# Dealing an expert's rows over all 128 partitions, and moving the small blocks as half rows

## The reference

```
top_val, top_idx = lax.top_k(logits, TOP_K)          # 4 of 32 experts for each of 512 tokens
top_w = jax.nn.softmax(top_val, axis=-1)
...
xb = h_pad[tok]                                      # rows of one expert
gu = xb @ w1[e] + b1[e]                              # 1024 -> 2048
gate = jnp.minimum(gate, SWIGLU_LIMIT)
up = jnp.clip(up, -SWIGLU_LIMIT, SWIGLU_LIMIT)
act = (up + 1.0) * (gate * jax.nn.sigmoid(SWIGLU_ALPHA * gate))
yb = act @ w2[e] + b2[e]                             # 1024 -> 1024
out = out.at[buf_tok].add(yb * wts)                  # back to the tokens
```

## Time and profile before

| | |
|---|---|
| median of 3 runs | 1963.04 us (1961.03 to 1964.29) |
| the profiled execution | 1963.06 us, span 1960.8 us, granted clock 0.99 |
| PE busy | 1857.0 us, 95% of the span |
| DVE, ACT, POOL busy | 1102.3, 942.7, 417.1 us |
| moved by DMA | 511.61 MB, mean 261 GB/s |

### The profile page before, as it was taken

The page is one execution under the profiler, slowest core; times in us unless marked ns, Lnnn a source line. Parts: engine busy times, 40 slices in busy tenths (PEclk is TensorE's granted clock), DMA queues, the critical chain, the costliest instruction groups (busy, mean ns, idle before and its releaser), DMA issues. The chain is left out here.

```text
span 1960.8 us, 27519 instructions
## 1 busy us (share of the span) xinstructions
PE 1857.0 (95%) x8716; PEld 1308.4 (67%) x8716; DVE 1102.3 (56%) x1354; ACT 942.7 (48%) x1342; POOL 417.1 (21%) x423
## 2 busy tenths in 40 slices
PE   7999999999999999997999999999999999999997
PEld 5887887887887888786655665556545655565553
DVE  6657657757757333456753564355445554564456
ACT  5666666666666222325443544344434443444341
POOL 0412421321320000012021233123322232223110
PEclk9999999999999999997999999999999999999998
DMA  5122122122131222366999999999999999999997
GB/s 182 65 89 87 65 88 99 54 88 99 64 108 57 97 97 96 131 238 230 369 403 415 414 403 402 409 409 405 402 411 405 405 404 406 407 402 404 406 397 325
DMA packets 88062, 511.61 MB, mean 261 GB/s; under 512 B 12882, under 2 KB 15994, under 8 KB 37720
## 3 DMA queue, kind: packets, MB, share of 16 engines
q1 hardware_dynamic: 80728, 492.70, 64.0%
q0 software_dynamic: 6720, 16.35, 2.4%
q10 hardware_dynamic: 576, 2.10, 0.3%
HBM read 502.08 MB, written 24.46 MB: 269 GB/s over the span
## 5 line engine op out<-in xcount | busy, mean ns | idle before, releaser
L2295 DVE TENSOR_TENSOR w_lo<-big,w_hi 128x2048 fp32r<-128x2048 f32 x141 | 322.1, 2292 | 354.3 <-ACT w_hi L2009 354.2
L2009 ACT ACTIVATE w_hi<-big 128x2048 fp32r<-128x2048 f32 x141 | 268.8, 1916 | 384.5 <-DMA big<-in_w 357.3
L1776 PE MATMUL bank<-big,keep 128*64 128x512 f32 x896 | 204.1, 600 | 0.0
L1197 PE MATMUL bank<-h_hi,wm_hi 128*128 128x512 f32 x416 | 171.1, 411 | 3.9 <-DVE big L918 2.4
L1197 PE MATMUL bank<-h_hi,wm_lo 128*128 128x512 f32 x416 | 163.0, 392 | 0.0
L1197 PE MATMUL bank<-h_lo,wm_hi 128*128 128x512 f32 x416 | 162.2, 390 | 0.0
L2295 DVE TENSOR_TENSOR w_lo<-keep,w_hi 128x2048 fp32r<-128x2048 f32 x48 | 110.0, 2294 | 71.4 <-ACT w_hi L2009 69.9
L1756 PE MATMUL bank<-w_hi,x_hi 128*128 128x512 f32 x512 | 144.0, 403 | 3.8 <-DVE w_lo L2295 3.2
L1776 PEld LDWEIGHTS bank<-big,keep 128*64 128x64 f32 x896 | 60.2, 137 | 118.8 <-issue 118.8
L1756 PE MATMUL bank<-w_lo,x_hi 128*128 128x512 f32 x512 | 137.6, 390 | 0.0
L1756 PE MATMUL bank<-w_hi,x_lo 128*128 128x512 f32 x512 | 137.1, 389 | 0.0
(11 more groups left out here) (352 smaller groups left out, 3711.1 us busy)
## 6 DMA issues: line engine op xcount, KB each, us to landing
big<-in_w SPq DMA_DIRECT2D x289, 1024.0 KB, 15.4
keep<-in_w SPq DMA_DIRECT2D x95, 1024.0 KB, 14.2
big<-in_w_mix SPq DMA_DIRECT2D x72, 512.0 KB, 3.3
keep<-in_w_tail SPq DMA_DIRECT2D x44, 512.0 KB, 3.2
big<-y_tok SPq DMA_DIRECT2D x5, 1024.0 KB, 11.7
keep<-in_x SPq DMA_DIRECT2D x8, 512.0 KB, 6.6
keep<-y_tok SPq DMA_DIRECT2D x3, 1024.0 KB, 10.5
big<-in_w_tail SPq DMA_DIRECT2D x4, 512.0 KB, 3.7
```

The costliest lines, as they stand in the source:

```text
L1197: ins = pe.matmul(to[:], w[:, k], h[:, k], start=(k == 0 and w is hi and h is h_hi), stop=(k == KT - 1 and w is lo))
L1776: ins = pe.matmul(bank[2 * (c // 2)][r, :], x_s[:, n], raw[s][:, c * 512:(c + 1) * 512], start=False, stop=n == KT - 1)
L2009: act.activation(w_hi[:, s], raw[r], ACT.Copy).then_inc(hi_ready, 1)
L2295: dve.tensor_tensor(w_lo[:, s], raw[r], w_hi[:, s].bitcast(F32), ALU.subtract).then_inc(lo_ready, 1)
```

## The change

`CAP` becomes 128, so a big block has a slot in each partition. The number of a slot no longer is its partition's: `slot_no` is filled by an iota of four dimensions, which deals the rows out. Partition 64a + 32b + 4c + d (a, b in 0 and 1; c in 0 to 7; d in 0 to 3) gets slot number 1 + 8a + 64b + c + 16d. So rows 1 to 8 go to partitions 0, 4, ..., 28, rows 9 to 16 to 64, 68, ..., 92, rows 17 to 24 to 1, 5, ..., 29, and so on; rows 1 to 64 fill partitions 0 to 31 and 64 to 95, and rows from 65 on the other half.

A small block is gathered as 128 half rows of 2 KB: left halves to partitions 0 to 63, right halves to 64 to 127, each dealt in the same manner. Its eight transposes become four. Its results go out in one DMA of 128 half rows. Three small tables (`row_half`, `y_half_row`, `small_row`) hold the numbers for this; DVE fills them. The memsets of the edge from slot 112 to 128 go away, and the small DMA that doubled `cols` at the end, too. With blocks of 128 the overflow has 16 blocks at most, not 20.

```diff
-CAP, CS = 112, 64
+CAP, CS = 128, 64
-NOV = 20
+NOV = 16
+SMALL_ROWS = [(slice(32 * n, 32 * n + 32), slice(64 * (n % 2), 64 * (n % 2) + 32)) for n in range(4)]
...
+        h2_half = h2_rows.rearrange("r (h n) -> (r h) n", h=2)
...
                 def turn_x_s(b):

-                    for k in range(KT):
-                        ins = pe.transpose(bank[6][:, k * CS:(k + 1) * CS], xg_s[:, k * P:(k + 1) * P],
-                                           ident[0:CS, 0:CS])
+                    for k in range(4):
+                        ins = pe.transpose(bank[6][:, k * P:(k + 1) * P], xg_s[:, k * P:(k + 1) * P], ident)
...
+                for n, (to, of) in enumerate(SMALL_ROWS):
+                    ins = dve.tensor_scalar(row_half[to], rows[of, 0:E], 2.0, float(n // 2), ALU.mult, ALU.add)
+                ins.then_inc(halves_ready, 1)
...
-                    dve.tensor_scalar(halves[:, 0], slots[0:CS, 0:E], 2.0, None, ALU.mult)
-                    dve.tensor_scalar(halves[:, 1], slots[0:CS, 0:E], 2.0, 1.0, ALU.mult, ALU.add).then_inc(halves_ready, 1)
+                    for n, (to, of) in enumerate(SMALL_ROWS):
+                        dve.tensor_copy(small_row[to], rows[of, 0:E])
+                        ins = dve.tensor_scalar(y_half_row[to], slots[of, 0:E], 2.0, float(n // 2), ALU.mult, ALU.add)
+                    ins.then_inc(halves_ready, 1)
...
-                    pool.tensor_copy(ys_idx[:], halves[:, :, bass.ds(e, 1)].rearrange("p h a -> p (h a)")).then_inc(
-                        ysidx_ready.sem, 1)
+                    pool.wait_ge(halves_ready, 2)
+                    pool.tensor_copy(ys_idx[:], y_half_row[:, bass.ds(e, 1)]).then_inc(ysidx_ready.sem, 1)
...
-                    for h in range(2):
-                        pool.indirect_dma_start(y_half, bass.IndirectOffsetOnAxis(ap=ys_idx[:, h:h + 1], axis=0),
-                                                y_s[h * CS:(h + 1) * CS, :], None, bounds_check=2 * T * TOPK - 1,
-                                                oob_is_err=False).then_inc(yout_s.sem, 16)
+                    pool.indirect_dma_start(y_half, bass.IndirectOffsetOnAxis(ap=ys_idx[:, 0:1], axis=0), y_s, None,
+                                            bounds_check=2 * T * TOPK - 1, oob_is_err=False).then_inc(yout_s.sem, 16)
...
-                    gather(0, b, at, CAP, g_idx[:, 0:1], xg, gidx_ready, gather_b)
+                    gather(0, b, rows, at, g_idx[:, 0:1], xg, h2_rows, gidx_ready, gather_b)
...
-                    gather(1, b, e, CS, s_idx[0:CS, 0:1], xg_s, sidx_ready, gather_s)
+                    gather(1, b, row_half, e, s_idx[:, 0:1], xg_s, h2_half, sidx_ready, gather_s)
...
-                pool.iota(iota_i[:, 0:CAP], [[1, CAP]], base=1, channel_multiplier=0)
+                pool.iota(iota_i[:, 0:CAP], [[8, 2], [64, 2], [1, 8], [16, 4]], base=1, channel_multiplier=0)
...
-                for tile in (x_hi, x_lo, a_hi, a_lo):
-                    pool.memset(tile[:, :, CAP:P].bitcast(F32), 0.0).then_inc(edge_ready, 1)
-                pool.memset(pick_b[:, CAP:P].bitcast(F32), 0.0).then_inc(edge_ready, 1)
...
+                pool.wait_ge(halves_ready, 1)
                 gather_small(0, e_small)
...
-                pool.dma_start(cols[CS:2 * CS, 1:2], cols[0:CS, 1:2]).then_inc(cols_in, 16)
```

More of the change, by code:

```diff
@@ L401, in decoder_layer @@
                                                         sig("yrows_ready"))
-        yout_b, yout_s = sig("yout_b", 1, 16), sig("yout_s", 2, 16)
+        yout_b, yout_s = sig("yout_b", 1, 16), sig("yout_s", 1, 16)
         gidx_ready, sidx_ready, pickb_ready, picks_ready = (sig("gidx_ready"), sig("sidx_ready"), sig("pickb_ready"),
@@ L406, in decoder_layer @@
         fin_in = [Again(x_in[t], 32) for t in range(NT)]
-        cols_ready, cols_in, hot_last = sem("cols_ready"), sem("cols_in"), sem("hot_last")
+        cols_ready, hot_last = sem("cols_ready"), sem("hot_last")
         comb_ready, y_filled = sem("comb_ready"), sem("y_filled")
@@ L444, in decoder_layer @@
         key_row0, key_col0, e_col = yn[:, NID:NID + E], yn[0:E, NID + E:NID + E + 1], yn[0:E, NID + E + 1:NID + E + 2]
-        rt = Arena(keep, 9728)
+        rt = Arena(keep, 9856)
         rt.reset(8704)
@@ L469, in decoder_layer @@
         slots, rows = sb("slots", [CAP, NB], I32), sb("rows", [CAP, NB], I32)
-        halves = sb("halves", [CS, 2, E], I32)
+        row_half, y_half_row, small_row = (sb(name, [P, E], I32) for name in ("row_half", "y_half_row", "small_row"))
         blk_exp = sb("blk_exp", [P, NB + 1], I32)
@@ L476, in decoder_layer @@
         u_buf, s_buf = act_rows.rearrange("p (c n) -> p c n", c=2), ex.take(2, 512)[0:CAP]
-        xg_s = ex.take(D)[0:CS]
+        xg_s = ex.take(D)[:, 0:512]
         act_s, y_s, s_s = (ex.take(512) for _ in range(3))
@@ L488, in decoder_layer @@
         small_mem.reset(17920 + 2 * P)
-        x_s, a_s = small_mem.take(KT, CS), small_mem.take(4, P)
+        x_s, a_s = small_mem.take(4, P), small_mem.take(4, P)
         b12_raw = keep[:, 20480:20480 + D + 512]
@@ L497, in decoder_layer @@
                       Signal(z_ready.sem, base=HEADS * 4), Signal(sigz_ready.sem, base=HEADS * 4)]
-        g_idx, s_idx = sb("g_idx", [CAP, 1], I32), sb("s_idx", [CAP, 1], I32)
-        yb_idx, ys_idx = sb("yb_idx", [CAP, 1], I32), sb("ys_idx", [CS, 2], I32)
+        g_idx, s_idx = sb("g_idx", [CAP, 1], I32), sb("s_idx", [P, 1], I32)
+        yb_idx, ys_idx = sb("yb_idx", [CAP, 1], I32), sb("ys_idx", [P, 1], I32)
         ybidx_ready, ysidx_ready = (Signal(conv_ready.sem, base=HEADS * 4),
                                       Signal(silu_ready.sem, base=HEADS * 4))
-        edge_ready, bias_ready = sem("edge_ready"), sem("bias_ready")
+        bias_ready = sem("bias_ready")
         x_rows = x.rearrange("a s d -> (a s) d")
@@ L1775, in gate_up_s @@
                         r = slice(CS * (c % 2), CS * (c % 2 + 1))
-                        ins = pe.matmul(bank[2 * (c // 2)][r, :], x_s[:, n], raw[s][:, c * 512:(c + 1) * 512],
-                                        start=False, stop=n == KT - 1)
+                        ins = pe.matmul(bank[2 * (c // 2)][r, :], x_s[:, n % 4, CS * (n // 4):CS * (n // 4 + 1)],
+                                        raw[s][:, c * 512:(c + 1) * 512], start=False, stop=n == KT - 1)
                     ins.then_inc(s_used, 1)
@@ L1836, in body @@
                     step_b(j)
-                pe.wait_ge(edge_ready, 5)
                 pe.wait_ge(bias_ready, 2)
@@ L2357, in step_s @@
                         dve.wait_ge(cols_ready, 2)
-                        dve.wait_ge(cols_in, 16)
                         dve.tensor_tensor(diag_b, bcast_mid(ident, NT), bcast_inner(share_b, P), ALU.mult).then_inc(hot_last, 1)
@@ L2526, in carry_waits, with gather @@
                         spare_used[n].sem, 1)
[L2528 to L2532, removed]
+                def gather(n, b, table, at, idx, dst, src, ready, done):
+                    if isinstance(at, int):
+                        idx = table[:, at:at + 1]
+                        pool.sem_inc(ready.sem, 1)
+                    else:
+                        pool.tensor_copy(idx, table[:, bass.ds(at, 1)]).then_inc(ready.sem, 1)
+                        pool.wait_ge(ready.sem, ready.at(b, 1))
                     carry_waits(n, b)
-                    pool.indirect_dma_start(dst, None, h2_rows,
-                                            bass.IndirectOffsetOnAxis(ap=idx, axis=0), bounds_check=T - 1,
-                                            oob_is_err=False).then_inc(done.sem, 16)
+                    pool.indirect_dma_start(dst, None, src, bass.IndirectOffsetOnAxis(ap=idx, axis=0),
+                                            bounds_check=src.shape[0] - 1, oob_is_err=False).then_inc(done.sem, 16)
                 def scatter_b(b, at, n):
@@ L2633, in _ @@
                 pool.tensor_copy(cols[0:CAP, 0:1], rows[:, bass.ds(e_big, 1)])
-                pool.tensor_copy(cols[0:CS, 1:2], rows[0:CS, bass.ds(e_small, 1)])
+                pool.tensor_copy(cols[:, 1:2], small_row[:, bass.ds(e_small, 1)])
                 pool.iota(tok_i, [[1, T]], base=0, channel_multiplier=0).then_inc(cols_ready, 1)
```

## The result

The changed kernel takes 1927.47 us (median of 6 runs, 1926.59 to 1929.87) against 1963.47 us for the kernel before (6 runs, 1960.80 to 1964.73). The ratio is 0.9818, with a 95% interval of 0.9808 to 0.9829: 36.0 us less. The profiled execution took 1929.3 us with a span of 1927.4, 33.4 less than the span before; it is 1.8 us above the median of its kernel, so two microseconds of the 36.0 are not in the trace that follows.

What follows compares the result with a forecast made beforehand. The prediction took the DMA stream of weights as the bound, with PE up to 4.2 us a pair below. Gathers -23.0, deal -8.8 and beginning +0.3 make -31.5 us, from 1963.06 to 1931.5 us; range 1923 to 1951.

Steps and rivals of the forecast that it cites:

- the 37 us: Steady part of the loop: 37.0 us lost against 423 GB/s, 25.5 for gathers and 11.5 for rows dealt unevenly over engines.
- The gathers: Expert blocks' gathers: rows landing in on-chip memory slow the weights; the change recovers 90% of 25.5 us, 23.0 us.
- The deal: Rows of a block fall unevenly on the 16 DMA engines; evening them out recovers 8.8 of 11.5 us.
- Half rows, fewer scatters, POOL: Small block's half rows, one scatter for two, longer lists on POOL: nothing; other bound for half rows 8 us.
- PE, beginning, end: PE's pair stays at 60.4 us; new DVE operations at the beginning add 0.3 us; end nothing, within 1 us.
- What would show it: Signs: periods 62 to 62.6 us, gathers at 400 GB/s or more, late stretches at 420, PE's two waits under 2 us.
- The read rival: Gathers are slow by reading scattered rows and stay so; only the deal gains, 9 to 12 us, about 1953; chance 0.13.
- the price of half rows: Rival for the small block: half rows or longer lists take 8 us back, 1940; chance 0.06.
- The cut by eight neighbours: Rival: an engine's share of a tile is eight neighbouring partitions each; the kernel gets slower; chance 0.08.
- A cut by every 16th partition: Example of the rival of no change: fullest share 326 rows, gathers collide as before, 2.5 us less.
- The prediction's cut: One engine's share is partitions 4c to 4c+3 and 32+4c to 32+4c+3, same from 64 on; fullest has 271 rows.
- the no-change case: Rival: some cut in between, gathers collide as before; 15 x 0.167, 2.5 us less, within 0.2%; chance 0.05.

Runs made afterwards that it cites:

- plain order: Changed kernel with 128 slots, but slot n in partition n, not dealt out: 1941.89 us, ratio to before 0.9892.
- the small block alone: Kernel before (112 slots, slot n in partition n) with only the small block's gather and scatter as 128 half rows: 1950.87 us, ratio 0.9940.
- the deal in between: Changed kernel with slots dealt in turn over the two halves of the partitions, following the partitions within a half: 1937.99 us, ratio 0.9878.

## Why the prediction was right, and where its sizes were off

**What bounds the kernel.** Right. The rate of the transfers set the pace and PE had some 4 us a pair to spare: with the rate at 421 to 422 GB/s the pair takes 62.2 us (forecast 62.3), and without the rows PE sets it at 60.28 (forecast 60.4).

**The split of the 37 us.** The loop gave back 33.7 us for the forecast's 31.8. By the medians of the runs, from before to the changed kernel: small gather 12.4 us; then the big block over 128 partitions for 112, still in plain order, 1950.87 - 1941.89 = 9.0 us; then the dealt order for the plain one, 14.4 us. The sum is 35.8 us beside 36.0, which it has to be, since these are steps between the same two kernels; it proves nothing. The loops of the traces give 14.4, 7.3 and 12.0 us for the same steps, together the 33.7. The middle step may mix two things, the big gather's clean landing and whatever 128 partitions in plain order change in the shares, and no run parts them. So:

- *The gathers*, forecast 23.0 us as 90% of 25.5. The small one is measured, 12.4 us by the medians and 14.4 by the loops, where the windows of one pair make 13.6 for 14 pairs. The big one, 14.3 by such windows, is not measured on its own; its step brought 9.0 and 7.3 us, and its window went from 351 to 415 GB/s. The windows at 422 and 415 leave next to nothing to be lost, so the discount of 10% looks too large. That it is the form in which the rows land and not the read is shown by the small gather in two DMAs: same reads, 352 GB/s. What collides there is not shown: no trace tells which engine wrote to which partition.
- *The deal*, forecast 8.8 us of 11.5: no run shows this term, since it rests on how the rows of the kernel before fell on the engines. What the runs showed in its place is the price of the plain order over 128 partitions, 14.4 us by the medians and 12.0 by the loops, and the big block's landing and the deal together: 36.0 - 12.4 = 23.6 us by the medians, 33.7 - 14.4 = 19.3 by the loops. Less the window estimate of 14.3 for the big gather, the deal is left with some 9 or 5 us, an estimate that is no better than the windows' edges. A row that goes out occupies its engine for 0.167 us by the prediction's estimate; 0.143 to 0.148 is felt by the medians, 0.12 by the loops. At these prices the 22 rows that the fullest share still has above the mean are worth 3 us, and against 423 GB/s the stretch loses 871.1 - 867.2 = 3.9.
- That the two add up was assumed, and the runs agree with it: the small block's landing is worth 12.4 us with the plain order and 13.3 with the even deal (14.4 and 13.1 by the loops). For the big gather this wasn't tried: no run has an even deal with the big block over 112 partitions.
- Of the 4.5 us by which the forecast of 31.5 fell short, 2 us are the difference between the profiled execution and the median; what they are stays open.

**Half rows, fewer scatters, POOL.** Right at nothing: the changed kernel's small gather of 128 half rows passes at 422 GB/s, and the second scatter was worth 1.5 us by the medians, hardly more than their spread, one issue at the end included. POOL's timeline has the last scatter of the changed kernel, for the two of the earlier trace rows:

```profile
1870.40 1.04 POOL L2560 DMA_INDIRECT y_tok<-keep,ys_idx  x1 [0.54 <-issue]
```

It ends at 1871.4 us, 0.5 behind the last L1743; before, the second one ended 1.9 behind (1906.7 for 1904.8).

**PE, beginning, end.** PE's pair is 60.3 for 60.4. The new operations at the beginning, in DVE's timeline:

```profile
897.15 0.71 DVE L2291 TENSOR_SCALAR row_half<-rows 32x32 int32<-32x32 int32 x4
```

They take 0.71 us for the 0.9 allowed, and the first pair starts at 939.5 us as before, for a forecast of +0.3. The end is 0.5 us longer, forecast 0 within 1.

**What would show it.** Periods between 61.2 and 62.8 us with a mean of 62.2; gathers at 400 GB/s or more; late stretches at 422; PE's two waits together 1.6 us in the pair shown, 1.3 in the mean: each as said.

**The rivals.** The read rival is excluded by the small gather in two DMAs, the price of half rows by the 422 GB/s in their window. The cut by eight neighbours is excluded by the orders of slots: by it the fullest shares of the changed kernel, the deal in between and the plain order would be 362, 372 and 372 rows, so the first two would differ by 10 rows, some 1.4 us; they differ by 10.5 us. A cut by every 16th partition would give 326, 304 and 277 rows and put the three the other way round. The prediction's cut (partitions 4c to 4c + 3 with 32 + 4c to 32 + 4c + 3) gives 271, 342 and 372, and the times are 1927.5, 1938.0 and 1941.9 us; of the cuts reckoned here it is the only one that fits. The 15 rows of the no-change case, like the 8.8 us of the sum, are reckoned against a fullest share of the kernel before, which no run shows; the change measured is 36.0 us.

## What to carry to other kernels

Where a stream of weights bounds the kernel, cut the span into windows by what else is in flight, and look also at the windows in which nothing else is: here a deficit there that grew over the first rounds went away with an even order of the slots, and its price followed the estimated fullest share, not the mean or the number of full ones. Give side transfers that write on-chip memory the same form over the partitions as the stream's tiles have, even if that means half rows and longer lists: here the small gather moved 422 GB/s so, for 352 as two DMAs of 64 partitions. Before working on the rest, let a run without the side traffic show the next bound: here PE stands 27 us below, and what is left of the rows is mostly their bytes, 14.42 MB or, as an estimate, 34 us at 421 GB/s.

## What the runs showed of the hardware

- One core, the only one that this kernel runs on, sustained 421 GB/s for 871 us; no window shown of the changed kernel's loop is below 415.
- A gather over 64 or 112 partitions pulled the rate of the whole stream down to 351 to 358 GB/s while it landed (320 in one window of before), about 1 us each; 1 MB of weights took 46 to 50 us of engine time beside a small one, for 39. Over 128 partitions gathers passed at 410 to 422. Windows with a big block's scatter show 423 to 433, over 112 partitions or 128, and two scatters for one cost 1.5 us by the medians, with ranges that overlap.
- The loss by the uneven deal followed the fullest share, as it is estimated above, and not the number of engines that have it: by that count 71 rows more on two engines cost 10.5 us, 101 more on six cost 14.4 (8.2 and 12.0 by the loops).
- In the stretch of 14 pairs the skipped entries of a list cost nothing that could be measured: q0 had 6153 packets, where it has 6128 with the rows, but they held 0.04 MB and took 0.4% of the engines, and PE didn't wait once.
- The granted clock fell to half (0.51 in the window shown) for 3.4 us at a time, six times in the loop of the plain order and eight times in that of the small block alone, and the pairs in which it did so were no longer than the others: where the transfers set the pace, PE had room for it.
